# The last expert scatter summed with x in PSUM, and two norms folded into one turning factor

## The reference, cut to what matters

```python
# end of the first block
x = x + gt2 * expert_choice_ffn(h, w_router, w_gate, w_up, w_down)
x = rms_norm(x, g_final)            # x * rsqrt(mean(x*x) + 1e-6) * g_final
# start of the second block, layer 0
h = rmsnorm(x, mix_norm_g[0])       # the same form, another gain
x = x + mixing_layer(h, ...)        # first step: h @ w_in[0]
```

## Time and profile before

| | us |
|---|---|
| median of 3 runs | 2751.97 |
| the profiled execution's own time | 2751.75 |
| its span in the trace | 2750.0 |

### The profile page before, as it was taken

How to read it: one execution, slowest core, us unless ns; L and a number is a source line. 1 busy time by engine, 2 the same in 40 slices (tenths; PEclk the granted TensorE clock), 3 DMA queues, 4 the chain that set the end, 5 groups by cost and what they waited for, 6 DMA issues and landing times.

```text
span 2750.0 us, 35540 instructions
## 1 busy us (share of the span) xinstructions
PE 2666.7 (97%) x14516; PEld 1992.7 (72%) x14516; DVE 990.3 (36%) x1810; ACT 824.6 (30%) x1455; POOL 784.5 (29%) x633
## 2 busy tenths in 40 slices
PE   7999999999999999999999799999999999999998
PEld 4777777886568884444444596988888987988887
DVE  3655566523522133212222497410011686300012
ACT  3444444322433231000000326422222336322222
POOL 2222233310114400000000242444445442344454
PEclk9999999999999999999999999999999999999999
DMA  7112221011204316999999421222322221222321
GB/s 269 55 62 74 82 64 61 31 35 52 67 25 134 117 69 265 383 422 426 426 425 426 182 87 47 77 92 92 99 100 92 78 86 37 93 92 92 108 92 46
DMA packets 189046, 382.41 MB, mean 139 GB/s; under 512 B 11889, under 2 KB 146933, under 8 KB 163317
## 3 DMA queue, kind: packets, MB, share of 16 engines
q1 hardware_dynamic: 187568, 379.07, 37.3%
q10 hardware_dynamic: 1349, 1.51, 0.2%
HBM read 378.46 MB, written 2.10 MB: 138 GB/s over the span
## 4 chain that ended last, share of the span: by engine, by line
PE 83%; DMA 8%; DVE 3%; ACT 2%; issue 1%; DVEq 1%; SPq 0%; ACTq 0%; POOL 0%; PEld 0%; PEldq 0%
PE bank L1609 14%; PE bank L1614 14%; PE bank L1613 14%; PE bank L1884 7%; PE bank L1377 5%; DMA ring<-in_w_up 4%; DMA ring<-in_w_gate 3%; PE bank L1827 2%; PE bank L1768 2%; PE bank L1411 2%; PE bank L1473 2%; PE bank L1482 1%; PE bank L1486 1%; PE bank L1663 1%; PE bank L1392 1%
## 5 line engine op out<-in xcount | busy, mean ns | idle before, releaser
L705 POOL TENSOR_TENSOR w_lo<-ring,w_hi 128x512 fp32r<-128x512 f32 x448 | 603.1, 1378 | 1449.6 <-ACT w_hi L753 1449.6
L753 ACT ACTIVATE w_hi<-ring 128x2048 fp32r<-128x2048 f32 (+1 forms) x114 | 215.0, 1886 | 668.4 <-PE bank L1609 668.3
L1609 PE MATMUL bank<-hT_hi,w_hi 128*128 128x512 f32 (+1 forms) x928 | 352.1, 379 | 2.9 <-DVE conv_acc L2792 1.6
L1614 PE MATMUL bank<-hT_hi,w_lo 128*128 128x512 f32 (+1 forms) x928 | 347.8, 375 | 0.0
L1613 PE MATMUL bank<-hT_lo,w_hi 128*128 128x512 f32 (+1 forms) x928 | 347.6, 375 | 0.0
L1884 PE MATMUL bank<-ring,xeT 128*64 128x512 f32 x992 | 224.9, 596 | 12.1 <-DMA ring<-in_w_gate 5.7
L1609 PEld LDWEIGHTS bank<-hT_hi,w_hi 128*128 128x128 f32 x928 | 174.8, 188 | 35.2 <-DVE conv_acc L2792 2.4
L1614 PEld LDWEIGHTS bank<-hT_hi,w_lo 128*128 128x128 f32 x928 | 174.7, 188 | 31.7
L1613 PEld LDWEIGHTS bank<-hT_lo,w_hi 128*128 128x128 f32 x928 | 174.8, 188 | 30.8 <-issue 1.0
L2885 DVE TENSOR_TENSOR ffn_hT<-ffn_sg,bank 128x512 f32<-128x512 f32 x44 | 30.2, 687 | 414.8 <-PE bank L1614 414.8
L1884 PEld LDWEIGHTS bank<-ring,xeT 128*64 128x64 f32 x992 | 74.7, 136 | 136.9 <-issue 136.5
(11 more groups left out here) (506 smaller groups left out, 4872.8 us busy)
## 6 DMA issues: line engine op xcount, KB each, us to landing
ring<-in_w_gate SPq DMA_DIRECT2D x86, 1024.0 KB, 7.9
ring<-in_w_down SPq DMA_DIRECT2D x86, 1024.0 KB, 13.4
ring<-in_w_up SPq DMA_DIRECT2D x82, 1024.0 KB, 13.4
ring<-in_w_in SPq DMA_DIRECT2D x33, 1024.0 KB, 5.2
head_w<-in_w_in SPq DMA_DIRECT2D x32, 512.0 KB, 4.8
mod_w<-in_w_mod SPq DMA_DIRECT2D x8, 2048.0 KB, 7.7
ring<-in_w_out SPq DMA_DIRECT2D x12, 1024.0 KB, 4.7
ring<-in_w_mod SPq DMA_DIRECT2D x8, 1024.0 KB, 15.9
```

The costliest lines, as they stand in the source:

```text
L705: last = pool.tensor_tensor(w_lo[m % 2][:, cs], src[:, cs], w_hi[m % 2][:, cs].bitcast(F32), ALU.subtract)
L753: return act.activation(dst, src, ACT.Copy)
L1609: first = mm(dst, a[0], b[0], start=start, stop=False)
L1614: return mm(dst, a[1], b[0], start=False, stop=stop)
```

## The change

Everything lies between the last expert pair and the first projections of block 2.

- TensorE first writes x itself into the banks, by products with the identity (four for tiles 0 and 1, then two each for tiles 2 and 3), and lets the scatter add to it. Each tile has its own pair of banks.
- VectorE no longer adds. It multiplies the bank by `g_final` into x. The first norm's factor is left out of x at this point.
- ScalarE sums three kinds of squares for each tile: of the two banks (the first norm) and of the gained x (the second). With s the first norm's mean square plus epsilon and q the mean square of the gained x, both factors together are 1/sqrt(q + eps*s); VectorE forms eps*s (`half_eps`) in tiny instructions. `diag` holds this joint factor.
- The first factor alone is still wanted for x. GpSimd multiplies it in, a 128x1024 instruction for each tile, once the tile has been taken: tiles 0 and 1 ahead of chunk 1's remainder, tiles 2 and 3 ahead of chunk 2's.
- The order is new. VectorE and ScalarE take tiles 0 and 1 through to `hT_lo` before they begin on tiles 2 and 3. TensorE turns tiles 0, 1, 2, makes the first block's early projection, and turns tile 3 behind it. ScalarE splits chunk 1 last.
- ScalarE's table load for the root and two small copies come ahead of the last `ye_hi`.

```diff
 # GpSimd
+            def scale_by_root(t):
+                pool.wait_ge(sem("h_ready"), 2 * t + 2)
+                pool.tensor_tensor(x[:, t, :], x[:, t, :], rstd[:, 4 + t:5 + t].to_broadcast([P, DM]), ALU.mult)
             for l in range(LAYERS):
                 for m in range(PER_LAYER):
+                    if l == 0 and m in (1, 2):
+                        scale_by_root(2 * m - 2)
+                        scale_by_root(2 * m - 1)
                     pool.wait_ge(hi_ready, MERGES + l * PER_LAYER + m + 1)
                     remainder(m, raw[m % RAW])
 # ScalarE
-            split_ye(PAIRS - 1)
             reached(act, "block2_consts")
             copy(ident_r[:], ident[:])
             copy(causal_r[:], causal[:]).then_inc(step["mask_parts"], 1)
+            act.activation(root_junk[:, 0:1], eps_col[:, 0:1], ACT.Sqrt)
+            split_ye(PAIRS - 1)
...
             split(0)
-            act.activation(sq_junk[:, 0:1], eps_col[:, 0:1], ACT.Sqrt)
-            for t in range(TT):
+            def moe_sums(t):
+                act.wait_ge(sem("scattered"), (PAIRS - 1) * 8 + 2 * t + 2)
+                act.drain()
+                act.activation(sq_junk[:, 512:1024], bank[2 * t + 1][:], ACT.Square, accum_out=ss[:, 8 + t:9 + t]).then_inc(sem("moe_rms"), 1)
+                act.wait_ge(sem("x_added"), (PAIRS - 1) * 8 + 2 * t + 1)
+                act.activation(sq_junk[:, 0:512], bank[2 * t][:], ACT.Square, accum_out=ss[:, 4 + t:5 + t]).then_inc(sem("moe_rms"), 1)
                 act.wait_ge(sem("x_added"), (PAIRS - 1) * 8 + 2 * t + 2)
                 act.drain()
-                tile_rms(4 + t, t, "moe_rms")
-                if t:
-                    tile_sum(0, t - 1)
-                if t >= 2:
-                    tile_hi(0, t - 2)
-            tile_sum(0, TT - 1)
-            tile_hi(0, TT - 2)
+                act.activation(sq_junk[:], x[:, t, :], ACT.Square, accum_out=ss[:, t:t + 1])
+                act.drain()
+                act.wait_ge(sem("x_tile"), TT + t + 1)
+                act.activation(rms[:, t:t + 1], ss[:, t:t + 1], ACT.Sqrt, scale=1.0 / DM, bias=half_eps[:, t:t + 1])\
+                    .then_inc(sem("rms_ready"), 1)
+                act.activation(rms[:, 4 + t:5 + t], half_ss[:, t:t + 1], ACT.Sqrt, scale=1.0 / DM, bias=eps_col[:, 0:1])\
+                    .then_inc(sem("moe_rms"), 1)
+            moe_sums(0)
+            moe_sums(1)
+            tile_hi(0, 0)
+            tile_hi(0, 1)
+            moe_sums(2)
+            moe_sums(3)
+            tile_hi(0, 2)
+            tile_hi(0, 3)
             split(1)
-            tile_hi(0, TT - 1)
 # TensorE
-            for piece in range(8):
-                if piece >= 4:
-                    pe.wait_ge(sem("x_added"), (PAIRS - 1) * 8 + piece - 3)
-                scatter(PAIRS - 1, piece, bank[piece % 4][:])
+            def x_into_banks(t):
+                for hf in range(2):
+                    mm(bank[2 * t + hf][:], ident[:], x[:, t, hf * 512:(hf + 1) * 512], start=True, stop=False)
+            x_into_banks(0)
+            x_into_banks(1)
+            for t in range(TT):
+                if t >= 2:
+                    x_into_banks(t)
+                for hf in range(2):
+                    scatter(PAIRS - 1, 2 * t + hf, bank[2 * t + hf][:], fresh=False)
...
-                b0 = 2 * t if n and n % 2 == 0 else 2 * (t % 2) + (0 if n else 4)
-                if t >= 2 and (n % 2 or not n):
+                b0 = 2 * t if n % 2 == 0 else 2 * (t % 2)
+                if t >= 2 and n % 2:
...
-            for t in range(TT):
+            for t in range(3):
                 turn_tile(0, t)
             first_projection(0, 0)
+            turn_tile(0, 3)
 # VectorE
-            def moe_scaled(t):
-                dve.wait_ge(sem("moe_rms"), t + 1)
+            def moe_gained(t):
+                dve.wait_ge(sem("scattered"), (PAIRS - 1) * 8 + 2 * t + 1)
+                tt(x[:, t, 0:512], bank[2 * t][:], gfin_b[:, 0:512], ALU.mult).then_inc(sem("x_added"), 1)
+                dve.wait_ge(sem("moe_rms"), 3 * t + 1)
+                tt(x[:, t, 512:1024], bank[2 * t + 1][:], gfin_b[:, 512:1024], ALU.mult).then_inc(sem("x_added"), 1)
+                dve.wait_ge(sem("moe_rms"), 3 * t + 2)
+                ts(half_eps[:, t:t + 1], ss[:, 4 + t:5 + t], EPS / DM, EPS * EPS, ALU.mult, ALU.add)
+                tt(half_ss[:, t:t + 1], ss[:, 4 + t:5 + t], ss[:, 8 + t:9 + t], ALU.add)
+                dve.drain()
+                stt(half_eps[:, t:t + 1], ss[:, 8 + t:9 + t], EPS / DM, half_eps[:, t:t + 1], ALU.mult, ALU.add)
+                dve.drain().then_inc(sem("x_tile"), 1)
+            def joint_diag(t):
+                make_diag(0, t)
+                dve.wait_ge(sem("moe_rms"), 3 * t + 3)
                 dve.reciprocal(rstd[:, 4 + t:5 + t], rms[:, 4 + t:5 + t])
-                dve.drain()
-                stt(x[:, t, :], x[:, t, :], rstd[:, 4 + t:5 + t], gfin_b[:], ALU.mult, ALU.mult)
-                dve.drain().then_inc(sem("x_tile"), 1)
             dve.wait_ge(sem("row_b_in"), 64)
-            for t in range(TT):
-                for piece in (2 * t, 2 * t + 1):
-                    add_scattered(PAIRS - 1, piece, bank[piece % 4][:])
...
+            moe_gained(0)
+            moe_gained(1)
+            joint_diag(0)
+            take_tile(0, 0)
+            joint_diag(1)
+            tile_lo(0, 0)
             take_tile(0, 1)
             tile_lo(0, 1)
-            make_diag(0, 3)
-            for t in (2, 3):
-                take_tile(0, t)
-                tile_lo(0, t)
+            moe_gained(2)
+            moe_gained(3)
+            joint_diag(2)
+            take_tile(0, 2)
+            joint_diag(3)
+            tile_lo(0, 2)
+            take_tile(0, 3)
+            tile_lo(0, 3)
```

More of the change, by code:

```diff
@@ L1843, in slots_of, with scatter @@
                 last.then_inc(sem("slots_done"), 1)
-            def scatter(pair, piece, dst):
+            def scatter(pair, piece, dst, fresh=True):
                 t, hf = piece // 2, piece % 2
@@ L1852, in scatter @@
                 rows, cols = scat_now[:, t * P:(t + 1) * P], slice(hf * 512, (hf + 1) * 512)
-                mm(dst, rows, ye_hi[:, cols], start=True, stop=False)
+                mm(dst, rows, ye_hi[:, cols], start=fresh, stop=False)
                 mm(dst, rows, ye_lo[:, cols], start=False, stop=True).then_inc(sem("scattered"), 1)
@@ L2698, in moe_scaled @@
+            def joint_diag(t):
+                make_diag(0, t)
+                dve.wait_ge(sem("moe_rms"), 3 * t + 3)
                 dve.reciprocal(rstd[:, 4 + t:5 + t], rms[:, 4 + t:5 + t])
-                dve.drain()
-                stt(x[:, t, :], x[:, t, :], rstd[:, 4 + t:5 + t], gfin_b[:], ALU.mult, ALU.mult)
-                dve.drain().then_inc(sem("x_tile"), 1)
             dve.wait_ge(sem("row_b_in"), 64)
-            for t in range(TT):
-                for piece in (2 * t, 2 * t + 1):
-                    add_scattered(PAIRS - 1, piece, bank[piece % 4][:])
-                if t:
-                    moe_scaled(t - 1)
-                if t >= 2:
-                    make_diag(0, t - 2)
-                if t == 3:
-                    take_tile(0, 0)
-                    tile_lo(0, 0)
@@ L2714, in _ @@
-            moe_scaled(3)
-            make_diag(0, 2)
+            moe_gained(0)
[4 more added lines that the diff above has]
+            tile_lo(0, 0)
             take_tile(0, 1)
             tile_lo(0, 1)
-            make_diag(0, 3)
-            for t in (2, 3):
-                take_tile(0, t)
-                tile_lo(0, t)
+            moe_gained(2)
+            moe_gained(3)
+            joint_diag(2)
+            take_tile(0, 2)
```

## The result

The changed kernel takes 2760.37 us (median of 11 runs, 2755.63 to 2762.4), the kernel before beside it 2751.63 us (2751.1 to 2757.87). The ratio is 1.0028, 95% interval 1.002 to 1.0036: slower by 7.7 us (5.5 to 9.9); the medians themselves differ by 8.7 us. Forecast was 2758.7. Three executions of 5990 to 9904 us, two of the kernel before and one of early_scaled, are left out of all ratios. The span of the profiled execution is 2758.6 us, against 2750.0.

The account below looks back on a forecast made before the run. TensorE, busy 97% of the span, was taken as the bound. Tile 2's turn at 1560.4 plus 17.55 us puts the second chunk at 1577.95 against 1571.08: +6.9 us, forecast 2758.7 us, range 2753.5 to 2761.5.

Parts of the forecast that it names:

- x into the banks: On TensorE before the first scatter: eight instructions take 3.44 us, so the scatter starts 1.2 us later (bounds 0 and 2.9).
- Table load: On ScalarE: the load and two small copies fit its idle 18.3 us ahead of ye_hi and cost nothing.
- Sums of tiles 0 and 1: On ScalarE: 3.35 us a tile, one tiny VectorE instruction held, tile 0's turn at 1543.2 against 1544.49 before.
- The hold: VectorE waits for GpSimd's scalings of tiles 0 and 1 to end, costing 4.0 us (bounds 0 and 4.6).
- Tiles 2 and 3 only behind tile 1: VectorE reaches these tiles late, called the main loss; 6.0 us of steps put tile 2's turn at 1560.4.
- Clock: TensorE restarts at 1.2 GHz after a 10 us gap, for 3.3 to 5.5 us; 2.2 us lost (1.65 to 2.75).
- From there to T1: TensorE from tile 2's turn to the second weight chunk: turns, projection products and clock loss, 17.55 us, ending at 1577.95.
- Turn 3 later, at nothing: On TensorE: turning tile 3 behind the first block's early projection costs nothing extra, as its diagonal is ready near 1565.1.
- Remainder 1 level with T1: GpSimd's remainder of chunk 1 ends at 1577.4 to 1578.3, level with TensorE's second chunk, adding 0 to 0.3 us.
- Rivals 3 and 4: Rival 3 (0.12): low half of chunk 2 late, 1.0 us stall, 2759.9 us; rival 4 (0.04): faster, VectorE sheds scalings.
- Rival 1: GpSimd's scalings do not hold VectorE: only +2.9 us, 2754.8 us; chance 0.26.
- rival 2: TensorE's clock holds because it is fed from 1531.7 to 1550: +4.7 us, 2756.7 us; chance 0.06.

Follow-up runs that it names:

- early_scaled: Changed kernel with vec_scaled's and both_early's edits, tile 3's diagonal made before tile 2 is taken, chunk 1 split last; ratio 0.9997 to the kernel before.
- vec_scaled: Changed kernel with the scaling of x moved from GpSimd to VectorE, behind the last tile_lo and chunk 1's remainder; ratio 1.001 to the kernel before.
- both_early: Changed kernel with the early halves of both blocks of the first projection ahead of turns 2 and 3; ratio 1.0023 to the kernel before.
- turn3_first: Changed kernel with tile 3 turned ahead of the first projection again, as before the change; one time, 2760.31 us.
- clock_held: Changed kernel with 38 products of the identity with itself on TensorE between turns 1 and 2; ratio 1.0019 to the kernel before.
- after_again: The changed kernel itself, run and profiled again with nothing altered; ratio 1.0024 to the kernel before.
- joined: vec_scaled with both_early, tile 1's x into banks behind tile 0's scatter, tile 3's diagonal before taking tile 2, chunk 1 split before last two tile_hi; ratio 1.0008.
- split_first: early_scaled with ScalarE splitting chunk 1 right behind chunk 0; ratio 1.0018 to the kernel before.

## Why the prediction was right

Its steps in order, measured from ye of each trace.

- *x into the banks.* Eight instructions took 3.69 us for the predicted 3.44. The first scatter starts 0.9 us later from ye, predicted 1.2 (its upper bound of 2.9 should read 2.5: eight times 0.59 from 1531.7, less 1533.95); the sums on ScalarE began at ye + 4.8, predicted ye + 4.7.
- *Table load.* No cost showed: it ran at 1516.21, and ScalarE had nothing else to do until 1533.99.
- *Sums of tiles 0 and 1.* One tiny instruction held for 1.16 us, as counted. Turn 0 at ye + 10.9, predicted ye + 11.5: 0.6 too late.
- *The hold.* Predicted 4.0 us, measured by removing it (vec_scaled) as 4.2 at turn 2, 4.5 against the second profile. The size is near, its division was not: the working has some 2 us for the diagonal and 2 for tile 1's hT_lo. The diagonal lost 1.62 us (1.91 - 0.29) and tile 1's hT_lo 1.51 (2.98 in the changed kernel, 1.47 in vec_scaled), 3.1 together. Tile 0's hT_lo, which the list of signs has as stretched, was not (1.27): it began when the scaling was over. The other 1.1 us came by way of TensorE: behind the gap of 2.84 us made by the late diagonal the clock fell in turn 1 (3.13 against 2.05 us), so the second bank of tile 1 was late. The prediction has no such term, and it differs between executions: none in both_early, 0.5 us in turn3_first, 1.7 in clock_held. That the sum came so near to 4.0 is partly luck.
- The hT_lo pair ended 0.55 us behind the scaling's end, about one instruction of its own. The Trainium skill ("SBUF — State Buffer", section "SBUF: two separate sides") calls this an exclusive lock, and names two kinds of VectorE instruction that take part: those with two SBUF inputs and those in what it calls a 2-port perf mode. The trace agrees for hT_lo, which has two such inputs. The prediction names only this kind; the diagonal reads one 128x128 block and a column and waited too (1.91 us), so if the rule covers it, it is by the second kind, which no run here tests.
- *Tiles 2 and 3 only behind tile 1.* Turn 2 at ye + 28.2, predicted ye + 28.7. That "this order is the main loss" is not borne out: with the hold gone and the order kept, T1 was 1.3 us behind the kernel before (vec_scaled), where the working leaves 2.9. The hold was the larger part, 4.9 to 5.3 us at T1.
- *Clock.* Half clock for 5.4 us from the restart, 2.7 us lost where 2.2 was taken: the upper end of the range. In after_again it was 3.9 us, 1.9 lost.
- *From there to T1.* 17.7 us, predicted 17.55. T1 - ye +6.6, predicted +6.9.
- *Turn 3 later, at nothing.* It cost nothing, and by the estimate above it saved TensorE a wait of about 1.2 us.
- *Remainder 1 level with T1.* It ended 0.14 us before T1. Rivals 3 and 4 did not occur: scalings 2 and 3 took 3.75 us and delayed nothing of TensorE's, end - T1 is +0.4.
- Rival 1 (no hold) is refuted by the 1.91 and 2.98 us rows and by vec_scaled, rival 2 (the clock holds) by the 0.50 slices.

The mechanism was the predicted one: GpSimd's scalings hold VectorE, tile 2 is turned late, and the clock falls in the wait. The time came out 1.7 us above the forecast. In the profiled execution 1.5 us lie ahead of ye, where the code is nearly the same (0.5 in after_again, where ye is 1532.19); whether the medians hold the same share the runs don't show.

## What to carry to other kernels

Before work is given to an idle GpSimd, look at what VectorE does in that stretch: here a 2 us GpSimd instruction on SBUF cost a diagonal of 0.29 us another 1.6 us and a pair of hT_lo 1.5 us, and four scalings that took GpSimd 7.9 us took VectorE 2.74. Let TensorE begin with the tiles that are ready first only if it is then fed with that work (both early halves here), since otherwise the wait for the rest and the clock's fall are both paid. Fill TensorE's gaps where TensorE itself is waited for behind them; ahead of work that others set the pace of, the fill brought nothing here. And before a difference of 1 or 2 us in one trace is put down to an edit, compare how long the clock was down in both.

## What the runs showed of the hardware

- 128-column products of the identity, two instructions of 0.13 us, brought the clock back to full while nothing else ran (clock_held: 0.50 at 1553 to 1554, 1.00 from 1554) and kept it there.
- The clock fell within a gap of 2.26 us in early_scaled (0.79 at 1550 to 1551, where the gap ends at 1550.61) and not in the same gap of joined. Behind the same gap of 2.84 us turn 1 took from 2.05 us (both_early, full clock) to 3.78 (clock_held, half clock). In the gap of 7.77 us of vec_scaled the clock was 1.00 for the first 3.8 us. The runs don't tell what decides.
- GpSimd's scaling of 128x1024 by a column took 1.89 us, where twice the 512-wide instruction of the earlier trace rows gives 2.09 (the prediction has 2.07). VectorE does the same work in 0.69 us (four in 2.74).
- Beside GpSimd's w_lo or scalings, VectorE's instructions with two SBUF inputs and the diagonal were held: 128x1 in 1.14 to 1.17 us for 0.16, the diagonal in 0.93 to 1.91 for 0.29. Beside w_lo these were not: a reciprocal of 128x1 (0.16 us in split_first, 1542.31) and products that read a PSUM bank (0.69 us).
